# Attention of an even block: who copies the turned probabilities, and who sums the squares of the attended rows

## What is computed

```python
def diff_attention(q, k, v, lam):          # 4 heads, two maps m of 64 channels, 1280 keys, values of 128
    def one_block(qblk):                   # 128 queries
        s = einsum('bqhmd,bkhmd->bhmqk', qblk, k) * ATTN_SCALE
        p = softmax(s, axis=-1)
        a = p[:, :, 0] - lam * p[:, :, 1]
        return einsum('bhqk,bkhv->bqhv', a, v)

ao = rms_norm(attn_o, subln_g) * (1.0 - lam_init)      # over the 128 values of a head
```

## Time and profile before

| what | value |
|---|---|
| median of three runs | 1809.46 us (1807.63 to 1817.28) |
| span of the profiled execution | 1803.4 us (its own time is not printed beside it) |
| busy: TensorE, VectorE, ScalarE, GpSimd | 1742.9, 1212.7, 800.6, 759.5 us |
| attention: first scores to last copies of the turned rows | about 359.6 to 593 us |
| in 360 to 600 of it | TensorE 213, VectorE 209, ScalarE 166, GpSimd 18 us busy of 239 |

### The profile page before, as it was taken

How to read it: one execution, slowest core, us unless ns; L and a number is a source line. 1 busy time by engine, 2 the same in 40 slices (tenths; PEclk the granted TensorE clock), 3 DMA queues, 4 the chain that set the end, 5 groups by cost and what they waited for, 6 DMA issues and landing times.

```text
span 1803.4 us, 22828 instructions
## 1 busy us (share of the span) xinstructions
PE 1742.9 (97%) x8677; PEld 1461.8 (81%) x8677; DVE 1212.7 (67%) x1390; ACT 800.6 (44%) x1253; POOL 759.5 (42%) x450
## 2 busy tenths in 40 slices
PE   6999999989998899999999999999999999999999
PEld 4788887888888688788888889978888888878887
DVE  3734799578898616854545743786666667689865
ACT  3522222667677325533333432754435444444443
POOL 2332422000001142466666520548999999810000
PEclk8999999999999999999999999999999999999999
DMA  9567123000000731222221611303232232286433
GB/s 358 204 216 238 48 83 117 4 24 1 0 0 1 245 106 47 59 82 59 60 81 59 198 59 47 117 24 106 82 93 83 72 92 82 85 329 223 147 122 123
DMA packets 165385, 188.32 MB, mean 104 GB/s; under 512 B 9454, under 2 KB 117543, under 8 KB 165159
## 3 DMA queue, kind: packets, MB, share of 16 engines
q1 hardware_dynamic: 165287, 187.00, 31.7%
HBM read 152.37 MB, written 34.60 MB: 104 GB/s over the span
## 4 chain that ended last, share of the span: by engine, by line
PE 53%; DVE 4%; ACT 2%; issue 1%; DMA 1%; SPq 0%; ACTq 0%; DVEq 0%
PE ps L3217 20%; PE ps L2225 15%; PE ps L3268 10%; PE ps L2285 5%; PE ps L3568 1%; PE ps L3230 1%; DVE cv_lo_p L132 1%; DVE up_lo_p L132 1%; DVE residual L2147 0%; ACT residual L3404 0%; PE ps L3234 0%; DVE residual L3126 0%; DMA w_raw<-in_ffn_w_out 0%; ACT cv_hi_p L129 0%; ACT residual L1964 0%
## 5 line engine op out<-in xcount | busy, mean ns | idle before, releaser
L3217 PE MATMUL ps<-up_hi_p,st_hi_p 128*128 128x512 f32 x560 | 218.7, 391 | 2.9 <-ACT residual L2935 2.9
L3217 PE MATMUL ps<-up_lo_p,st_hi_p 128*128 128x512 f32 x560 | 218.5, 390 | 0.0
L3217 PE MATMUL ps<-up_hi_p,st_lo_p 128*128 128x512 f32 x560 | 218.3, 390 | 0.0
L3268 PE MATMUL ps<-down_ring 128*128 128x512 f32 x924 | 210.9, 390 | 2.8 <-DVE down_ring L132 2.6
L3268 PEld LDWEIGHTS ps<-down_ring 128*128 128x128 f32 x924 | 173.0, 188 | 40.5 <-issue 4.0
L132 POOL TENSOR_TENSOR in_lo<-in_raw,in_hi 128x512 fp32r<-128x512 f32 (+1 forms) x54 | 96.9, 1803 | 215.5 <-ACT in_hi L129 215.5
L2225 PE MATMUL ps<-cv_hi_p,cv_st_hi_p 128*128 128x512 f32 x392 | 153.2, 391 | 2.7 <-ACT residual L1943 2.7
L2225 PE MATMUL ps<-cv_hi_p,cv_st_lo_p 128*128 128x512 f32 x392 | 153.0, 390 | 0.0
L2225 PE MATMUL ps<-cv_lo_p,cv_st_hi_p 128*128 128x512 f32 x392 | 153.0, 390 | 0.0
L2067 DVE TENSOR_TENSOR residual<-ps,residual 128x512 f32<-128x512 f32 x70 | 48.3, 691 | 120.0 <-PE ps L2225 120.0
L132 POOL TENSOR_TENSOR st_lo_p<-up_raw,st_hi_p 128x512 fp32r<-128x512 f32 x68 | 101.7, 1499 | 64.4 <-ACT st_hi_p L129 64.4
(11 more groups left out here) (396 smaller groups left out, 4232.4 us busy)
## 6 DMA issues: line engine op xcount, KB each, us to landing
up_raw<-in_ffn_w_in SPq DMA_DIRECT2D x44, 512.0 KB, 5.0
w_raw<-in_ffn_w_out SPq DMA_DIRECT2D x66, 256.0 KB, 2.8
cv_raw<-in_odd_w_in SPq DMA_DIRECT2D x32, 512.0 KB, 5.5
in_raw<-in_even_w_in SPq DMA_DIRECT2D x48, 256.0 KB, 3.9
y_scratch<-residual SPq DMA_DIRECT2D x22, 512.0 KB, 2.6
ada_raw<-in_ada_w SPq DMA_DIRECT2D x16, 512.0 KB, 9.1
square<-in_ada_w SPq DMA_DIRECT2D x16, 512.0 KB, 4.3
rest_odd<-in_ada_w SPq DMA_DIRECT2D x16, 512.0 KB, 4.4
```

The costliest lines, as they stand in the source:

```text
L3217: last = pe.matmul(ps[:, bank(j, p), :], w[p][:, kk * P:(kk + 1) * P], x[p][:, kk, :], start=(first and w is st_hi and x is up_hi), stop=( ...
L3268: last = pe.matmul(ps[:, 4 * (i % 2) + m, :], slot[:, s, m * P:(m + 1) * P], slot[:, x, :], start=(k == 0 and s == 0 and x == 2 and DOWN[i ...
```

## The change

VectorE no longer copies round 0, save for the very last tile (`turn_out_last`). ScalarE copies all three rounds of a tile one after the other (`rounds_out`), at the place where it copied rounds 1 and 2: ahead of the exponentials of tile t, it copies the rounds of tile t-2. The copy of round 0 also takes over the wait for the values of two tiles before (`o_done`), which frees its half of `mixed_t`.

`finish` only scales. The squares of heads 0 to 2, and of tiles 0 to 3 of head 3, go to GpSimd (`squared`), which multiplies the scaled rows of a whole head by themselves and adds halves, 64, 32, ... 1 wide, into `o_stat`: eight dependent instructions. They stand in GpSimd's loop behind the doubled columns of the next head. Tiles 4 to 7 of head 3 keep their squares on ScalarE (`finish_squared`). The roots wait for GpSimd's sums.

```diff
+                            if i == 0:
+                                act.wait_ge(sem("o_done"), n - 1 + CREDIT)
                             act.activation(mixed_t[:, t % 2, b * P:e * P],
...
                             act.wait_ge(sem("o_done"), n + 1 + CREDIT)
-                            src = out_of(h, t)
-                            act.activation(o_all[:, h, t, :], src, ACT.Copy, scale=inverse[:, t, 0:1])
-
-                            act.wait_ge(sem("o_scaled"), n + CREDIT)
-                            act.activation(o_square[:, :], src, ACT.Square, scale=inverse[:, t, 0:1],
-                                           accum_out=o_stat[:, h, t:t + 1]).then_inc(sem("o_scaled"), 1)
-
-                        def last_rounds(h, t):
-                            for i in range(1, 3):
+                            act.activation(o_all[:, h, t, :], out_of(h, t), ACT.Copy, scale=inverse[:, t, 0:1])\
+                               .then_inc(sem("o_scaled"), 1)
...
+                        def rounds_out(h, t):
+                            for i in range(3):
                                 turn_out(h, t, i)
 
                         def tiles(h):
                             for t in range(2, RT):
-                                last_rounds(h, t - 2)
+                                rounds_out(h, t - 2)
                                 for m in range(2):
                                     exps(h, t, m)
                                 if t < L1:
-                                    finish(h, t - 2)
+                                    (finish_squared if isinstance(h, int) and t - 2 >= SQUARED_BY_POOL else finish)(h, t - 2)
...
                             tiles(h)
+                            turn_out(h, L2, 0)
                             for m in range(2):
                                 high_k(act, h + 1, m, score[m])
...
                             finish(h, L2)
-                            last_rounds(h, L1)
+                            rounds_out(h, L1)
...
+                        def squared(h, end):
+
+                            pool.wait_ge(sem("o_scaled"), h * RT + end + CREDIT)
+                            rows, squares = o_all[:, h, 0:end, :], o_square[:, 0:end, :]
+                            pool.wait_ge(sem("o_summed"), h * SUMS_OF_HEAD + CREDIT)
+                            pool.tensor_tensor(squares, rows, rows, ALU.mult).then_inc(sem("o_summed"), 1)
+                            for i in range(1, SUMS_OF_HEAD):
+                                n = DV >> i
+                                to = squares[:, :, 0:n] if n > 1 else o_stat[:, h, 0:end].unsqueeze(2)
+                                pool.wait_ge(sem("o_summed"), h * SUMS_OF_HEAD + i + CREDIT)
+                                pool.tensor_tensor(to, squares[:, :, 0:n], squares[:, :, n:2 * n], ALU.add)                                    .then_inc(sem("o_summed"), 1)
+
+                        with pool.Fori(0, HEADS - 1) as h:
                             for name, dst, src in (("k", k_head, k_nat), ("q", q_head, q_nat)):
 
-                                pool.wait_ge(sem(name + "_turned"), h * 2)
+                                pool.wait_ge(sem(name + "_turned"), (h + 1) * 2)
...
+                            squared(h, RT)
+                        squared(HEADS - 1, SQUARED_BY_POOL)
...
                             combine(h1, t1)
                             peaks(h, t, 1)
                             combine_rest(t1)
-                            turn_out(h1, t1)
```

More of the change, by code:

```diff
@@ L356, in program @@
                 q_head = sb(heads, "q_head", [P, 2, RT, 2, DH])
-                o_square = sb(heads, "o_square", [P, DV])
+                last_square = sb(heads, "last_square", [P, DV])
                 o_stat = sb(heads, "o_stat", [P, HEADS, RT])
@@ L368, in program @@
                              for m in range(OUT_FIRST)]
+                o_square = sb(behind, "o_square", [P, RT, DV])
             out_raw = []
@@ L521, in program @@
         CREDIT = 2
-        credited = ["mixed", "mixed_rest", f"mix_turned{LAST}", f"mix_copied{LAST}", "o_done", "o_scaled"]
+        SUMS_OF_HEAD, SQUARED_BY_POOL = 8, 4
+        credited = ["o_summed", "mixed", "mixed_rest", f"mix_turned{LAST}", f"mix_copied{LAST}", "o_done", "o_scaled"]
         credited += [x + state for x in "kq" for state in ("_twice", "_turned", "_high", "_low")]
@@ L937, in _ @@
                         tiles(HEADS - 1)
-                        finish(HEADS - 1, L2 - 1)
-                        last_rounds(HEADS - 1, L2)
-                        last_rounds(HEADS - 1, L1)
+                        finish_squared(HEADS - 1, L2 - 1)
+                        rounds_out(HEADS - 1, L2)
+                        for i in range(1, 3):
+                            turn_out(HEADS - 1, L1, i)
                         def heads_rooted(first, end):
-                            act.wait_ge(sem("o_scaled"), end * RT + CREDIT)
+                            act.wait_ge(sem("o_summed"), end * SUMS_OF_HEAD + CREDIT)
+                            if end == HEADS:
+                                act.wait_ge(sem("o_squared_last"), RT - SQUARED_BY_POOL)
                             act.activation(o_stat[:, first:end, :], o_stat[:, first:end, :], ACT.Sqrt, bias=eps[:, 0:1],
@@ L947, in _ @@
                         heads_rooted(0, HEADS - 1)
-                        finish(HEADS - 1, L2)
-                        finish(HEADS - 1, L1)
+                        finish_squared(HEADS - 1, L2)
+                        finish_squared(HEADS - 1, L1)
                         heads_rooted(HEADS - 1, HEADS)
@@ L965, in _ @@
                         pool.wait_ge(sem("y_f_done"), F_GROUPS)
-                        with pool.Fori(1, HEADS) as h:
+                        def squared(h, end):
[9 more added lines that the diff above has]
+                        with pool.Fori(0, HEADS - 1) as h:
                             for name, dst, src in (("k", k_head, k_nat), ("q", q_head, q_nat)):
-                                pool.wait_ge(sem(name + "_turned"), h * 2)
+                                pool.wait_ge(sem(name + "_turned"), (h + 1) * 2)
                                 for m in range(2):
-                                    pool.tensor_copy(dst[:, m, :, :, :], head_columns(src, h, m))\
+                                    pool.tensor_copy(dst[:, m, :, :, :], head_columns(src, h + 1, m))\
                                         .then_inc(sem(name + "_twice"), 1)
+                            squared(h, RT)
+                        squared(HEADS - 1, SQUARED_BY_POOL)
                         for m in range(OUT_FIRST):
@@ L1523, in combine_rest, with turn_out_last @@
                             mix(t, BANK, KEYS).then_inc(sem("mixed_rest"), 1)
-                        def turn_out(h, t):
-                            n = h * RT + t
+                        def turn_out_last():
+                            n = HEADS * RT - 1
                             b, e = rounds[0]
                             dve.wait_ge(sem("mix_turned0"), n + 1)
+                            dve.wait_ge(sem("mix_copied0"), n)
                             dve.wait_ge(sem("o_done"), n - 1 + CREDIT)
-                            dve.tensor_copy(mixed_t[:, t % 2, b * P:e * P], ps[:, 0 if is_last(h, t) else MIX_BANK, 0:(e - b) * P])\
-                               .then_inc(sem("mix_copied0"), 1)
+                            dve.tensor_copy(mixed_t[:, L1 % 2, b * P:e * P], ps[:, 0, 0:(e - b) * P]).then_inc(sem("mix_copied0"), 1)
                         def tile_step(h, t, h1, t1):
```

10 lines of the change are left out of this document (8 added, 2 removed).

## The result

The changed kernel takes 1826.04 us (median of four runs, 1825.53 to 1826.9) against 1808.84 for the kernel before (the three runs of 1809.46 and a fourth of 1808.22): 17.2 us slower, ratio 1.009 with a 95% interval of 1.0073 to 1.0106. The forecast was 1823, range 1811 to 1832. In a later set of runs (e9) the changed kernel stood at 1824.14 beside 1811.36, 12.8 us slower, ratio 1.007 (1.0045 to 1.0095).

What follows compares the result with a forecast made beforehand. A chain over two tiles, through VectorE's copy, was taken as the bound, TensorE 0.1 behind. Chain 7.0, passages 1.7, last head 0.5 and GpSimd's holds 4.6 made 13.8 us on 1809.5: about 1823, range 1811 to 1832.

Steps and rivals of the forecast that it cites:

- The bound as a loop over two tiles: Attention tiles: a chain through VectorE's copy and TensorE spans two tiles; 5.775 us a tile before, 6.065 after.
- the 7.0 us: Tile loops of four heads: ScalarE's copy behind the scaling makes each of 24 tiles 0.29 us longer.
- The passages: Three passages to a next head: turn1 (TensorE's transposes of blocks 4 to 7) starts 0.58 us later each, 1.7 us.
- Head 3: Last head: output weights' high parts and two squares lengthen the link, less VectorE holds saved by late low parts; +0.5 us.
- GpSimd beside VectorE: Heads 1 to 3: GpSimd's squares hold VectorE's weights or mixes, 3.8 us, and moved column copies 0.8; sum 4.6.
- the row at 374.21: Profile row before the change: a weight took 0.22 us beside a GpSimd plain copy; used to price moved copies at 0.8.
- The sum of 13.8: Whole kernel: tile chain 7.0, passages 1.7, last head 0.5 and GpSimd's holds 4.6 us, added to the median 1809.5.
- The signs: Profile after: copy directly behind scaling, turn1 waiting in nearly every tile, up to three long VectorE weights or mixes a head.
- (c): Attention tiles: VectorE's freed 0.68 us moves peaks forward, TensorE's 5.67 a tile rules; not slower, 1805 us; chance 0.10.
- (a): Attention heads: every meeting of GpSimd and VectorE a full one, 16.1 us in place of 4.6; 1835 us; chance 0.12.
- (b): Attention tiles: the longer chain is partly absorbed, GpSimd falls beside the peaks; 5 to 9 us, 1815 to 1818; chance 0.18.
- (d): Attention stage: TensorE's clock falls because its waits grow; left out of the sum, no chance of its own.

Runs made afterwards that it cites:

- e9: The changed kernel, unchanged, run and profiled again: 1824.14 us beside 1811.36 for the kernel before.
- e1: Only the copies against the kernel before: ScalarE copies all three rounds, the squares stay on ScalarE; 1824.63 us, ratio 1.007.
- e5: The changed kernel with ScalarE's copy of round 0 moved ahead of the scaling: 1818.86 us beside 1811.31 for the kernel before.
- e2: Only the squares against the kernel before: GpSimd squares and sums, VectorE copies round 0 as before; 1816.81 us, ratio 1.0022.
- e3: The changed kernel without GpSimd's sums of squares, the next head's columns doubled at the passage as before: 1823.0 us, ratio 1.0063.
- e4: The changed kernel with GpSimd's doubled columns of the next head ahead of the squares: 1826.58 us beside 1812.35 for the kernel before.
- e0: The kernel before, unchanged, profiled again: 1810.35 us (1811.31 beside it), span 1807.8.
- e8: The kernel before with nobody copying round 0, the values taking blocks 4 to 7 twice: 1802.75 us beside 1811.31, ratio 0.9954.

## Why the prediction was right

Step by step, with the trace of the changed kernel and the runs:

- **The bound as a loop over two tiles.** Right. It gave 5.775 for the kernel before, 6.065 for the change (measured 6.11), and its rule that a delay standing once in the loop costs half in a tile gives e1 (+0.18 for the square's 0.34 to 0.37) and e5 (-0.125 for the scaling's 0.24). What was off is one term: from a ScalarE copy to TensorE's start I took 0.05 from a row of the third round (561.61 to 561.66); for turn1 it is 0.15 (406.01 to 406.16), as it was behind VectorE's copy. Why the two rounds differ is open. That is the whole difference, 0.1 in a link and 0.05 in a tile, 1.1 us in 24 tiles. So the 7.0 us were 8.1.
- **The passages.** 1.7 foreseen, 1.1 measured: from the last turn1 of a head's loop to the first in the next head 20.03 us in place of 19.65 (412.20 to 432.23 against 408.34 to 427.99; 19.67 at the other two), three times 0.37. In e2, with the copy still on VectorE, the passage is 19.35. With the 0.32 us gained there, the 0.58 foreseen and the 0.1 of the start come to 0.36. That the square's leaving gives these 0.32 is likely, but no run has it alone.
- **Head 3.** 0.5 foreseen. e3 leaves 230.44 - 220.78 - 8.1 - 1.1 = 0.5 for it, but there the low parts don't queue behind the squares. In the changed kernel head 3 took 2.5 more, of which its seven intervals at 0.34 are 2.4: 0.1 is left for this term and for GpSimd's squares beside it together, where the sum had 0.5 and 1.25. The 1.7 kept of the held time is there (a mix of 128x768 took 2.71 us beside the low parts, 1.01 is usual).
- **GpSimd beside VectorE.** 4.6 foreseen, 1.9 to 2.5 measured (the tiles of the changed kernel less those of e3). The squares cost 2.2 and not 3.8: the product of a head took 1.89 and not 2.4, and the hold at the first addition was 0.9 (1.65 for 0.75), not 1.25. For the columns I had 0.8, and 0.3 was measured in heads 1 and 2 together, yet the step behind it failed: from the row at 374.21 I took that a plain copy hardly holds VectorE, and it does. The copy in that row ends within 0.2 us of the weight's start, and that overlap showed nothing. The rule of the Trainium skill's SBUF — State Buffer page, "Who interferes with whom", was the better guide to the hold. It was not to the time (2 us more by it), since most of the columns' hold is swallowed by the slack of the alternating tiles, which I hadn't put in the sum.
- **The clock.** Nothing foreseen. The end of the stage took 0.6 and 2.0 us more in the two profiles with the fall, and 0.5 less in e4 without it.
- **Total.** The sum of 13.8 stands against 12.8 to 13.5 in the stage. That it is so near is luck in part: the tiles had 1.1 too little and the clock up to 2.0, GpSimd over 2 and the passages 0.6 too much. The measured 17.2 has 4 us more, which lie outside the stage. e0 shows as much between two executions of the kernel before, with the clock behind the stage at 0.97 and 0.93, and in the later set of runs the loss was 12.8. I left the scatter of the rest of the kernel out of the sum, and the range held it. One reading was wrong without harm, since the sum starts from the median: I took 6.1 us as what lies around the span. Time and span of the changed kernel's profiled execution are 1.8 apart (1825.64 and 1823.8), so the profiled execution of the kernel before was some 4 us shorter than the median one.
- **The signs.** Scaling and copy follow at once (405.18, 405.42), and head 1 has three VectorE instructions over 1.2 us beside GpSimd (1.65, 1.69, 1.37). Turn1 showed a wait for the ScalarE copy in every tile of head 0's loop, but in 18 of 28 overall, not in nearly every tile. That VectorE holds GpSimd was named as a sign of being wrong: it does so for 0.46 us at the columns, beside holds of GpSimd on VectorE of 0.6 and 0.9.

The rivals: (c), that VectorE's relief moves the peaks forward, fell by the idle time before the peak, 0.38 to 1.2 us. e8 shows that even the whole copy for nothing gives 4 to 5 us in the stage. (a), every meeting a full one, fell with e3. (b) fell with the tile of 6.11. (d), the clock, which I gave nothing, has something in it: not within the tiles, since from 430 us to the last turn1 the granted clock is 1.00 in both kernels, but at the stage's end. That the change causes it is not shown.

## What to carry to other kernels

When work goes from a full engine to one with 25% idle time, ask where in that engine's queue it will stand and what stands in front of it. Here 0.60 us of work went behind an exponential and a scaling and made the link 0.67 us longer, in a loop that TensorE closes, while the spared engine only waited longer. Find the loop and count how many tiles it spans before pricing a delay: one that stands in a loop over two tiles costs half of itself in a tile. Compare a mended kernel with the old one mended the same way. And what is moved along on a third engine (here plain copies that left the passage for the tile loop) needs its own line in the sum.

## What the runs showed of the hardware that was not expected

A GpSimd plain copy from SBUF holds a VectorE instruction with two SBUF inputs as a tensor_tensor does: a weight of 0.22 us took 0.78, mixes of 0.75 took 1.69. A hold of 1.5 us in sum cost 0.2 us where tiles alternate. The product of equal inputs (128x1024) took GpSimd 1.89 us where an operation on two tiles took 2.36; that the equal inputs make the difference was not tried by itself. Behind equal waits of 2.1 us TensorE's clock stood at its lower level in two executions and at the higher one in a third. And 500 us behind the stage the granted clock over 120 us was 0.97 in one execution of the kernel before and 0.93 in another; the part behind the stage took 5.1 us more in the second, as much as many of the effects tested here.
